# Hybrid decoder step with a mixture of experts on one core: a skewed expert loop and a new ending

## What the kernel computes

```
def moe(h, ...):
    logits = t @ router_w + router_b
    vals, idx = lax.top_k(logits, 4)              # 4 of 32 experts
    gates = jax.nn.softmax(vals, axis=-1)
    for e in range(32):
        a = jnp.minimum(t @ w_gate[e] + b_gate[e], 7.0)
        u = jnp.clip(t @ w_up[e] + b_up[e], -7.0, 7.0)
        hid = (u + 1.0) * a * jax.nn.sigmoid(1.702 * a)
        y = y + combine[:, e:e + 1] * (hid @ w_down[e] + b_down[e])
x = x + mix
x = x + moe(rmsnorm(x, norm_ffn_w), ...)
y = rmsnorm(x, final_norm_w)
```

## Time and profile before

| what | value |
|---|---|
| median of three runs | 1128.1 us |
| the profiled execution | 1130.27 us |
| its span, from first to last instruction | 1128.4 us |
| mean granted TensorE clock | 0.994 |
| TensorE (PE) busy | 1103.0 us, 98% |
| VectorE (DVE) / ScalarE (ACT) busy | 394.5 us / 162.7 us |
| moved by DMA | 431.67 MB, mean 383 GB/s |

### The profile page before, as it was taken

One profiled execution on the slowest core, in us unless ns is written; L12 is line 12 of the kernel. 1 busy time (PEld: TensorE's weight loads), 2 busy tenths in 40 slices (PEclk: granted clock), 3 DMA queues, 4 the chain that ended last, 5 costly groups with the idle time before them and its releaser, 6 DMA issues.

```text
span 1128.4 us, 15518 instructions
## 1 busy us (share of the span) xinstructions
PE 1103.0 (98%) x6341; PEld 454.0 (40%) x6341; DVE 394.5 (35%) x703; ACT 162.7 (14%) x284; POOL 18.2 (2%) x45
## 2 busy tenths in 40 slices
PE   8999999999999999999999999999999999999997
PEld 5657754433333333333333333333333333333333
DVE  4165385433333333333333333333333333233233
ACT  3100124211111111111111111111111111111102
POOL 0002000000000000000000000000000000000000
PEclk9999999999999999999999999999999999999997
DMA  9970247999999999999999999999999999999991
GB/s 323 333 227 22 129 159 298 396 428 427 436 428 430 432 432 433 429 432 433 432 430 432 432 432 432 431 432 432 433 431 431 432 433 429 429 429 428 427 423 63
DMA packets 41442, 431.67 MB, mean 383 GB/s; under 512 B 3809, under 2 KB 23069, under 8 KB 26431
## 3 DMA queue, kind: packets, MB, share of 16 engines
q1 hardware_dynamic: 40592, 430.38, 91.3%
q10 hardware_dynamic: 815, 0.82, 0.2%
HBM read 427.48 MB, written 3.71 MB: 382 GB/s over the span
## 4 chain that ended last, share of the span: by engine, by line
PE 79%; DMA 19%; DVE 1%; ACT 0%; issue 0%; SPq 0%; DVEq 0%
PE ps L1428 47%; DMA ring<-in_w_gate 15%; PE ps L1135 9%; PE ps L1402 5%; DMA ring<-in_w_up 4%; PE ps L1254 3%; PE ps L1319 3%; PE ps L1411 2%; PE ps L1322 1%; PE ps L1390 1%; PE ps L1471 1%; PE ps L1125 1%; PE ps L1384 1%; DMA x<-in_x_sample 0%; PE ps L1511 0%; PE ps L1513 0%
## 5 line engine op out<-in xcount | busy, mean ns | idle before, releaser
L1428 PE MATMUL ps<-ring,RT 128*64 128x512 f32 x3072 | 689.8, 594 | 11.7 <-DMA ring<-in_w_gate 10.3
L1428 PEld LDWEIGHTS ps<-ring,RT 128*64 128x64 f32 x3072 | 210.5, 137 | 410.3 <-issue 381.7
L985 DVE SCALAR_TENSOR_TENSOR x<-ps,gates,x 128x1024 f32<-128x1024 f32 (+1 forms) x93 | 102.9, 1106 | 127.6 <-PE ps L1402 126.5
L1135 PE MATMUL ps<-R,ring 128*128 128x320 f32 x384 | 107.5, 436 | 0.3 <-issue 0.3
L991 DVE TENSOR_TENSOR RT<-ps,R 128x512 f32<-128x512 f32 x32 | 22.1, 692 | 228.9 <-ACT R L632 228.9
L1135 PEld LDWEIGHTS ps<-R,ring 128*128 128x128 f32 x384 | 71.8, 190 | 31.2 <-issue 1.8
L1402 PE MATMUL ps<-R 64*128 64x512 bf16 x558 | 76.8, 381 | 0.0
L1025 DVE TENSOR_SCALAR RT<-ps 128x512 f32<-128x512 f32 x32 | 22.1, 692 | 143.1 <-PE ps L1428 143.1
L624 ACT ACTIVATE RT<-RT 128x512 f32<-128x512 f32 x32 | 20.2, 630 | 300.1 <-DVE RT L1019 300.1
L1402 PEld LDWEIGHTS ps<-R 64*128 64x128 bf16 x558 | 20.8, 98 | 86.0 <-issue 50.3
L603 ACT ACTIVATE RT<-ps 128x512 f32<-128x512 f32 x33 | 19.7, 597 | 237.1 <-PE ps L1322 237.1
(11 more groups left out here) (226 smaller groups left out, 559.2 us busy)
## 6 DMA issues: line engine op xcount, KB each, us to landing
ring<-in_w_gate SPq DMA_DIRECT2D x26, 4096.0 KB, 32.5
ring<-in_w_up SPq DMA_DIRECT2D x25, 4096.0 KB, 32.0
ring<-in_w_down SPq DMA_DIRECT2D x25, 4096.0 KB, 32.8
ring<-in_w_up SPq DMA_DIRECT2D x14, 2048.0 KB, 39.0
ring<-in_w_down SPq DMA_DIRECT2D x13, 2048.0 KB, 39.8
ring<-in_w_gate SPq DMA_DIRECT2D x12, 2048.0 KB, 40.8
ring<-in_w_in SPq DMA_DIRECT2D x14, 1024.0 KB, 12.7
ring<-in_w_out SPq DMA_DIRECT2D x4, 1024.0 KB, 10.0
```

What stands on the lines that cost most here:

```text
L985: STT(xb[b], rows, gates[:, par, b:b + 1], xb[b], ALU.mult, ALU.add).then_inc(accDone, 1)
L1135: ins = MM(ps[:, n % 2, 0:NT], slot_k(L, 256)[:, k, 128 * half:128 * half + 128], hT[:, k, :], start=(k == 0), stop=(k == KT - 1))
L1428: ins = MM(shape(ps[64 * half:64 * half + 64, bank, :]), lhs(k), cols(w, half), start=False, stop=(k == KT - 1))
```

## The change

**Order of the products.** The down product of expert j is done after the up product of expert j + 1; the matrices are loaded in that order (g0 u0 g1 u1 d0 g2 u2 d1 ... g31 u31 d30 d31). `turn_gates` and `turn` are called between the quarters of the down product, the transposes of the hidden rows (`turn_hidden`) stand behind it, and the scatters of expert j - 2 stand in the gate product of expert j. `PT`, `eh` and `gates` get five buffers.

**Ending.** The last expert's output is kept in float32 (`yLast`, `PTLast`) and scattered in one float32 pass inside `one_round`. `final_norm_w` comes by DMA, spread over the partitions. `further_rounds` tests `rounds < 2` and holds the ending in both branches.

**Hand-over.** `choose(2)` goes ahead of `remainder(2, 0)`, `remainder(2, 1)` behind `place(2)`. The counts of tokens per expert get a semaphore and a bank of their own behind `positions(2)`; the matmuls over the earlier blocks move ahead of it. `gather_block(2)` waits for each of its three parts by itself.

```diff
+    I_GATE, I_UP, I_DOWN = [0] + [3 * j - 1 for j in range(1, E)], [1] + [3 * j for j in range(1, E)], [3 * j + 4 for j in range(E - 1)] + [MATS - 1]
...
-            with eng.If(rounds > 1):
+            with eng.If(rounds < 2):
+                ending()
+                eng.nop()
+            with eng.Else():
                 close_round(0)
...
+            def outputs():
+
+                sp.wait_ge(wUsed, 4 * NEXT + START)
+                sp.dma_start(fnw[0], A["final_norm_w"].partition_broadcast(128)).then_inc(fnwIn, 16)
+                for half in range(2):
+                    w = A["final_norm_w"][HALF * half:HALF * half + HALF]
+                    sp.dma_start(fnw[2][64 * half:64 * half + 64], w.partition_broadcast(64)).then_inc(fnwIn, 16)
...
+                        sigmoid(e)
+                        keep_rows(m, before)
+                        keep_slots(m, before * 3, buf(j + 1))
+                        act.wait_ge(wUsed, r * (LPE * E) + it * (LPE * PER_LOOP) + used_after(I_DOWN, j - 1) + START)
+                        act.wait_ge(scatMM, before * 3 + START)
                         act.activation(ysb[0], ps[:, 2, :], ACT.Copy).then_inc(yHigh, 1)
-                        act.wait_ge(yRest, e + 1 + START)
+                        keep_hidden(e)
+                        act.wait_ge(yRest, before + 1 + START)
                         act.activation(ysb[1], yrest, ACT.Copy).then_inc(yMid, 1)
...
+                act.activation(yLast, ps[:, 2, :], ACT.Copy).then_inc(yHigh, 1)
...
             keep_turned(2)
             norm_rows(2)
+            choose(2)
             remainder(2, 0)
-            choose(2)
-            remainder(2, 1)
             dve.wait_ge(xgMM, START)
             dve.wait_ge(gtMM, START)
             place(2).then_inc(prep, 1)
+            remainder(2, 1)
...
+                        gate_up(e, m, col, j, r * (LPE * E) + it * (LPE * PER_LOOP), rows)
+                        split_rows(e0 + (it * PER_LOOP + (j - 1)))
...
+                add_rows(p0 + (E - 2), e0 + (E - 2), buf(E - 2))
+                dve.wait_ge(yHigh, e0 + E + START)
+                dve.sem_inc(yLow, 1)
+                dve.sem_inc(yRest, 1)
+                add_rows(p0 + (E - 1), e0 + (E - 1), buf(E - 1), LAST)
...
             def gather_block(b):
-                pe.wait_ge(h2Parts, b + 1)
+                if b < 2:
+                    pe.wait_ge(h2Parts, b + 1)
                 for part in range(3):
+                    if b == 2:
+                        pe.wait_ge(*((partDone, 5), (partDone, 6), (h2Parts, 3))[part])
...
             gather_block(0)
             gather_block(1)
+            pe.wait_ge(posOut, 2)
+            earlier_blocks(2)
             stay_busy(2)
             positions(2)
+            counts()
             stay_busy(5)
...
+                def down(e, j, it, between):
+
+                    pe.wait_ge(yRest, e + START)
+                    product(2, half_c(hidT), I_DOWN[j], it, buf(j), between, operand=(hidTOut, e + 1 + START))
...
+                gate_up(e0, p0, 0, 0)
+                turn_hidden(e0)
+                turn_gates(p0 + 1)
+                turn(p0 + 1)
...
+                        gate_up(e, m, j, it, [lambda: None] + [lambda b=b: scatter(b, e2, m2, buf(j - 2)) for b in range(3)] if j > 1 else [])
+                        down(before, j - 1, it, [lambda: turn_gates(after), lambda: turn(after)])
+                        turn_hidden(e)
...
+                down(e0 + (E - 1), E - 1, 0, [lambda b=b: scatter(b, e0 + (E - 2), p0 + (E - 2), buf(E - 2)) for b in range(3)])
+                pe.wait_ge(ptLastOut, r + 1)
+                pe.wait_ge(yHigh, e0 + E + START)
+                pe.wait_ge(xgTOut, p0 + (E + 1) + START)
+                for b, (t0, n) in enumerate(TOK):
+                    if b == 1:
+                        pe.wait_ge(accDone, (e0 + (E - 1)) * 3 + START)
+                    for half in range(2):
+                        to = ps[:, LAST[b] + half, :] if b < 2 else ps[64 * half:64 * half + 64, LAST[b], :]
+                        ins = MM(to, PTLast[64 * half:64 * half + 64, t0:t0 + n], yLast[64 * half:64 * half + 64, :],
+                                 start=True, stop=True)
+                    ins.then_inc(scatMM, 1)
...
-            FN = 52
-            for k in range(D // 128):
-                row = ident[0:FN + 8, FN + k:FN + k + 1]
-                at = 128 * (k % 4)
-                MM(ps[:, 4 + k // 4, at:at + 128], row.broadcast_to([FN + 8, 128]), parRows[:], start=True, stop=True)
-                half = slice(64 * (k // 4), 64 * (k // 4) + 64)
-                ins = MM(ps[half, 2, at:at + 128], row.broadcast_to([FN + 8, 64]), parRows[:], start=True, stop=True)
-            ins.then_inc(fnwMM, 1)
```

More of the change, by code:

```diff
@@ L290, in further_rounds @@
                         eng.nop()
-                eng.nop()
-            with eng.Else():
+                ending()
                 eng.nop()
@@ L404, in _ @@
+            further_rounds(sp, all_loads, ending=outputs)
             sp.wait_ge(yOut, 64)
@@ L1029, in experts @@
[L1029 to L1034 removed]
+                        rows = (p0 + (it * PER_LOOP + (j - 2)), e0 + (it * PER_LOOP + (j - 2)), buf(j - 2)) if j > 1 else ()
+                        gate_up(e, m, col, j, r * (LPE * E) + it * (LPE * PER_LOOP), rows)
+                        split_rows(e0 + (it * PER_LOOP + (j - 1)))
@@ L1055, in _, with scales @@
-            for b in range(3):
-                dve.wait_ge(lastMM, b + 1)
-                rows = ps[:, LAST[b]:LAST[b] + 2, :].rearrange("p a n -> p (a n)") if b < 2 else ps[:, LAST[b], :]
-                STT(xb[b], rows, gates[:, buf(E - 1), b:b + 1], xb[b], ALU.mult, ALU.add).then_inc(moeDone, 1)
-            dve.wait_ge(moeDone, 3)
-            dve.wait_ge(fnwMM, 1)
-            for b in range(3):
-                final_scale(b)
+            def scales():
+                dve.wait_ge(fnwIn, 48)
+                for b in range(3):
+                    dve.wait_ge(finRoot, b + 1)
+                    dve.reciprocal(st[:, 6 + b:7 + b], st[:, 3 + b:4 + b]).then_inc(finScale, 1)
+                    dve.wait_ge(finScale, b + 1)
+                    STT(yout[:, b, 0:WIDE[b]], xb[b], st[:, 6 + b:7 + b], fnw[b], ALU.mult, ALU.mult).then_inc(finDone, 1)
@@ L1065, in _ @@
+            further_rounds(dve, one_round, rounds=rounds[0], ending=scales)
         @block.tensor
@@ L1461, in experts @@
-                        pe.wait_ge(xgTOut, m + START)
-                        pe.wait_ge(aDone, e + START)
-                        product(0, 0, half_c(xgT), e, it, j, [lambda: None] + [lambda b=b: scatter_before(b) for b in range(3)]
-                                if not isinstance(e, int) or e > 0 else [])
-                        pe.wait_ge(uDone, e + START)
-                        product(1, 1, half_c(xgT), e, it, j)
-                        gather(m)
-                        pe.wait_ge(hidDone, e + 1 + START)
@@ L1469, in experts @@
-                        pe.wait_ge(hidTOut, e + START)
-                        for c in range(4):
-                            ins = TR(ps[:, 4, 128 * c:128 * c + 128], fourth(hid, c), ident)
-                        ins.then_inc(hidTMM, 1)
-                        turn_gates(m)
-                        turn(m)
-                        pe.wait_ge(yRest, e + START)
-                        product(2, 2, half_c(hidT), e, it, j, operand=(hidTOut, e + 1 + START))
-                experts(0, range(FIRST))
+                        e, m = e0 + (it * PER_LOOP + j), p0 + (it * PER_LOOP + j)
```

310 lines of the change are left out of this document (162 added, 148 removed).

## The result

The changed kernel takes 1165.86 us (median; 1162.33 to 1166.96 in four runs) against 1128.63 (1128.0 to 1130.52) for the kernel before: a ratio of 1.0322, with a 95% interval of 1.0296 to 1.0347. The forecast was 1121.6, between 1120.0 and 1127.0, and faster. The direction was wrong.

What follows compares the result with a forecast made beforehand. Two close bounds, TensorE's own work and the weight stream: D 1109.6 plus 11.9 gave a span of 1121.5, 6.9 less than before. Taken off the 1128.1 median, plus 0.4 for the branch: 1121.6 us, range 1120.0 to 1127.0.

Steps and rivals of the forecast that it cites:

- D: End of the last down product on TensorE; forecast at 1109.6 us, 1.3 later than before.
- Thirty steps of 28.18: 1098.7: TensorE's expert loop: from gate 2 at 253.3, thirty experts of 28.18 us each, reaching 1098.7 us.
- rival 2: VectorE's jump over the further rounds: its gap stays, behind the adds, 2.1 to 2.5 us more, 1124; 11%.
- D later than 1112: Sign that the forecast is wrong: the last down product on TensorE ends after 1112 us.
- Rival 1: Cuts in the down product: TensorE becomes the bound and eats the gain; 10% for slower, 8% for 1125 to 1130.
- price per cut: Groups cutting into TensorE's products: up to 0.1 us to enter, 0.15 to resume; 0.43 taken per expert.
- P: TensorE's time for one expert in the new order: 27.75 + 0.43 = 28.18 us.
- gate 2: Start of expert 2's gate product on TensorE, the first without written-out experts ahead; forecast at 253.3 us.
- up 31's late half: Weight stream: late half of matrix 93, at 1083.96 us; the path from there ends the last down product at 1109.1.
- TensorE's own path: End of the last down product from TensorE's work without the weight stream: forecast 1108.9 us.
- The ending: From the last down product to the span's end: 11.9 us instead of 20.1, a gain of 8.2.
- The hand-over: Work ahead of TensorE's first gate product: 0.2 us earlier, bounds 0 and 0.8, start at 208.94 instead of 209.14.

Runs made afterwards that it cites:

- e1: The changed kernel with the head of TensorE's expert loop placed at slot 28 of a 256-instruction fetch block; 1125.73 us, ratio 0.9975.
- e7: The changed kernel with 24 small filler matmuls (48 instructions) added at TensorE's start, loop statement unchanged; 1126.34 us, ratio 0.9974.
- e9: The changed kernel with a hint at the back edge of TensorE's loop that it is taken; 1124.26 us, ratio 0.9956.
- e6: The kernel before with TensorE's loop head set to slot 230; median of ten runs 1140.27 us, from 1130.07 to 1157.48.
- e8: The kernel before with only `final_norm_w` by DMA, the 32 matmuls that spread it gone; 1125.69 us, ratio 0.9971.
- e10: The kernel before with `final_norm_w` by DMA, the test turned to `rounds < 2` and the ending in both branches; 1125.47 us, ratio 0.9963.
- e12: The changed kernel with TensorE's loop head at slot 215, 35 instructions in an eighth block; 1150.03 us, ratio 1.018.

## Why the prediction was wrong, point by point

**The step that failed** is one that I took for nothing. The sum for D has "Thirty steps of 28.18: 1098.7", with no term for the five jumps back, and the reason stands under rival 2: "against it: loops jump back without a gap in the expert's chain". In the changed kernel the jumps cost 42.2 us, and D came at 1149.76 instead of 1109.6. The trace of before showed a loop whose instructions weren't fetched again, and I carried it over to a loop with another place in the instruction stream. I costed the moved groups as matmuls and never asked where their instructions lie. e1, e7 and e9 each take about 40 us away without touching the work, and e6 brings the stops into the old order. The list of what would be wrong held the symptom (D later than 1112), not the mechanism.

By the Trainium skill (Runtime: NRT & Kernel Launch, Instruction fetch mechanics) TensorE's instruction memory holds 128 KiB, refilled in 16 KiB blocks, ahead in sequence only, and a jump out of the window waits for a DMA. The runs agree with the stops (1.3 to 3.3 us at the jumps, 66 packets) and with a store of that size: bodies in seven blocks of 16 KiB were not fetched again. They do not agree with the same section's sentence that the memory is "only 2 cache lines": in the kernel before, a body of 6.3 blocks ran through its passes from 387 to 1106 us without one packet of q8.

**Rival 1** had the right effect from the wrong cause: TensorE without slack passes everything on. Its price per cut was not the matter: the cuts together cost 0.38 us an expert, where 0.43 was forecast.

**P** was 28.13 (forecast 28.18), the first gate product 208.92 (208.94), gate 2 253.25 (253.3). **D**, freed of the stops, was right as well: e1's chain of waits at the end.

```profile
1041.48 42.37 DMA ring<-in_w_up
1083.89 3.65 PE ps L1496 x16
...
1109.42 0.74 issue
1110.16 1.14 PE ps L1565 x4
...
1111.39 1.29 DVE x L1036
...
1114.83 0.16 DVE st L1112
```

D is 1109.42 (forecast 1109.6), and the stream sets it: up 31's late half at 1083.9 (1083.96). TensorE's own path, 1149.76 less 42.2, would have ended at 1107.6 and not at 1108.9; thirty times 0.05 us in P are 1.5 of it.

**The ending** was too short in the forecast: D + 13.8 instead of D + 11.9. It splits so. First add D + 1.97 (forecast 1.6): the first float32 pair took 1.14 instead of 0.86 (over 1 us a pair was one of the signs of being wrong), and 0.1 more passed ahead of it. Adds to reciprocal 3.44 instead of 3.2. Reciprocal to the end 1123.2 - 1114.83 = 8.4 instead of 7.1. All four cases side by side, in us behind D:

| | first add | reciprocal | end of span |
|---|---|---|---|
| before | 5.4 | 13.0 | 20.1 |
| e8, weights by DMA | 5.4 | 8.6 | 15.7 |
| e10, and the branch turned | 3.4 | 6.5 | 15.8 |
| e1, the whole change without stops | 2.0 | 5.4 | 13.8 |

**Rival 2** (the gap at the jump stays, 2.1 to 2.5 more) was closer than its 11%: the gap didn't reappear behind the adds, but the branch's 2.2 us were lost again behind the outputs, where I had left 7.1 us unchanged. The float32 scatter in the new order takes 1.4 us off the first add, and the scatters of expert 30 put 1.3 on D. So of the whole change about the worth of the removed 32 matmuls stays: 20.1 - 15.7 = 4.4 us in the traces, 3.3 by e8's ratio.

Even without the stops the forecast's gain of 6.5 us was too large; e1 has 3.5 (1129.2 - 1125.73, the medians of its comparison). From the spans of the two profiled executions it is 1128.4 - 1123.2 = 5.2, the forecast 6.9 less 1.9 for the ending and 0.2 more for D. The rest is the base: the profiled execution of before, 1130.27, lies 1.1 above the median of 28 runs (1129.2), that of e1 0.7 below its own. I had seen the first gap, and took the whole difference off the median of three runs all the same.

**The hand-over** was worth 0.3 (forecast 0.2) at its place and nothing at the end.

## What to carry to other kernels

When an edit moves or lengthens an engine's instructions, look at the loop's own code as at a buffer: how many blocks it fills, where its head lies, and whether the queue of instruction fetches still falls silent once the passes run. Stops put down to "issue" right behind a jump back, and a count of instruction packets three times as high (66 instead of 22 here), are the sign; a shifted head or a hint at the back edge is the test and the cure in one line. Before a reordering is judged by its time, time it once with the loop shifted; else the placement is put down to the order.

And a gap moved out of the way has to be looked for where it can stand next, the outputs included.

## What had not been expected of the hardware

- The place of a loop's head alone was worth 40 us of 1126 (3.6%), with no instruction of the work changed: 1125.7 at slot 28, 1150.0 at 215, 1161.9 at 230, 1165.9 at its own place.
- The edge lies between 20 and 35 instructions in an eighth block: 20 gave 22 packets (30 and one stop in the order of before), 35 gave 67.
- A stop of about 3 us could cost more than itself: in e12 the granted clock fell to 0.50 at the first jump, and the gate product took 6.05 instead of 3.43 us; behind the last jump's stop of 3.10 it took 3.43.
- One packet of instructions 2 to 6 us ahead of the jump back went with every stop at it; profiles without that packet had none.
- The hint at the back edge (1124.26 us, 21 packets) kept a body in eight blocks from being fetched again in each pass, with the head at the same place. How it does that, the traces don't show.
